# A second stage whose first four weight units take x times the scales of both norms, with the norms' factor behind the bank

## The chip, the core and the metric

One core of a Trainium2 chip runs the whole program in one launch. The metric is the device time of one execution in microseconds (us), the median over several runs. All times in this text are in us unless marked ns. PE is the matmul engine (PEld its weight loads), DVE the vector engine, ACT the scalar engine, POOL GpSimd, SP the queue that loads the weights.

## The reference, cut to what matters

The program is a first block of two layers (feed-forward, mixer, feed-forward) on 256 tokens of width 1024, then a second block. The last operation of the first block is a norm with gain `final_g`; the second block begins with a norm and a modulation, and projects:

```
x = rms_norm(x, final_g)                        # end of the first block
h = _modulate(_rms_norm(x, g_norm_mix), sh1, sc1)
proj = h @ w_in                                 # (256 x 1024) @ (1024 x 3352)
r_q, r_k, r_v, r_g, n_q, n_kc, n_vc, n_ks, n_vs, n_kw, n_vw, n_gate = split(proj)
x = x + ga1 * mix                               # mix: retention and sparse attention of these
```

`_modulate(h, shift, scale)` is `h * (1 + scale) + shift`. Both norms divide each token by a root of its mean square, so for a token t and a channel c, h = x[t, c] * gain[c] * r[t] + shift[c], with one factor r[t] for both norms and one gain for both.

## The kernel before

**Layout and products.** Activations lie with channels on the 128 partitions, in KT = 8 tiles of 128 channels by 256 tokens (columns). Every fp32 product is made of three fp32r matmuls (`product`, lines 283 to 285): hi by hi, hi by lo, lo by hi, where hi is the value rounded to fp32r and lo is the rest. Weights stream in units of 128 x 1024 (512 KB) through a ring of four slots. For each half of a unit (0 and 1: four channel tiles each), ACT rounds it (`Stream.round`, line 175), DVE subtracts (`subtract`, line 182, or POOL from unit 10 of the second stage on, `subtract_beside`, line 235), and PE multiplies. There are two hi and two lo buffers, so that unit u can be rounded only when PE has used the same half of unit u-2 (the semaphore `used`). A unit of the second stage is `chunk` (line 192): 8 channel tiles by 3 matmuls of 256 columns. The first two units are a `pair` (line 258): for each channel tile, three matmuls into each of two banks, as the operand's tiles arrive.

**The end of the last feed-forward.** Its last eight units are products of six hidden tiles (18 matmuls each). Behind unit n, DVE adds the product to x (line 1173), ACT squares the tile of x (`square`, line 487), and PE sums the squares over channels into bank 7, twice, plain and with `final_g` squared (`DoubleNorm.sum`, line 600). The order is written out by hand in `Ffn.tensor`, `scalar` and `vector` (lines 1066 to 1184). `gather` (line 592) is empty for this norm.

**DoubleNorm and the start of the second stage.** PE issues 5 filler matmuls (`keep_warm`, line 385), the last sum, 6 fillers; DVE works out the means (613 to 615), ACT the root (621), DVE the reciprocal (626), and PE spreads the factor over the partitions by 4 matmuls (`spread`, line 633), then 7 fillers. Each filler and each spread appears as two instructions. Then for each channel tile DVE scales (`scale`, 544: x * gain * r into h), ACT rounds (553: h + shift into operand_hi) and DVE subtracts (`split`, 561: operand_lo), in `operands`, a scale ahead of each split. `Second.tensor` runs `pair` on units 0 and 1 (banks 0 and 6), then units 2 to 7 one by one. Their outputs are 128 channels each: compression keys, compression values, selection keys, window keys, four query tiles. ACT evicts each two units with one or two copies (lines 2043, 2044, 1959) and, behind the first two, makes four shifted copies of the compression values (`turned_values`, 1967 and 1968). DVE writes the normed x for the residual (`x2`, line 644), two tiles behind each of units 2 to 5. Behind unit 5 PE rotates the keys (`rotate`, line 1701) and DVE applies the positions (`rope`, 2135 to 2137). Units 8 to 15 are token-wise (activations as the stationary operand); from 16 on, units interleave with attention.

## Time and profile before

| | us |
|---|---|
| three runs | 2800.55, 2800.92, 2805.89 |
| median | 2800.92 |
| profiled execution, own time | 2799.17 |
| its span | 2797.3 |
| PE busy in the span | 2732.1 (98%) |
| end of the last feed-forward to the first product of the second stage | about 1751.4 to 1757.7 |
| mean granted clock of PE | 0.994 |

The profiled execution is 1.87 us over its span, and 1.75 us under the median. A timeline row gives the start from the span's start, the duration, engine, line, operation and tiles, the form and the count, and in brackets how long that engine had been idle and what released it. Rows of one instruction overlap the next where the engine is pipelined: what an instruction occupies is the distance from its start to the next start, and what a follower waits for is its end. PE rows that follow without a wait start 0.12 us apart for 256 columns, while each shows 0.28.

### The profile page before, as it was taken

Reading aid. Unit: us, or ns where it says so; the run is one execution under the profiler, and the core shown is the slowest. Engines: PE = TensorE matmul, PEld = TensorE weight load, DVE = VectorE, ACT = ScalarE, POOL = GpSimd, SP = SyncE. Lnnn points to the kernel's source line nnn. Section 1 sums busy time; section 2 is a strip of 40 time slices with the busy share of each in tenths; the row PEclk is TensorE's granted clock in tenths of the full one; section 3 lists DMA queues with packets and bytes.
Section 4 is the critical chain, followed back from the end, with each engine's and each line's share of the span. In section 5 each row is a group of like instructions: output and inputs, shape, how many; then the busy total and the mean of one; then the engine's idle time right before and its main releaser. Section 6 shows DMA issues by size and latency. Waiting matters only on the chain.

```text
span 2797.3 us, 40204 instructions
## 1 busy us (share of the span) xinstructions
PE 2732.1 (98%) x15618; PEld 2320.2 (83%) x15618; DVE 2067.0 (74%) x3773; ACT 1216.9 (44%) x2228; POOL 522.2 (19%) x449
## 2 busy tenths in 40 slices
PE   7999999999999999999988999999999999999998
PEld 5888878668888878888885999889999888888887
DVE  6989895568989896564766766765896677777776
ACT  5323233453232342222445545565556444444444
POOL 1111114300111101010050000345898000000000
PEclk9999999999999999999999999999999999999999
DMA  7555533223555445354441566424654556655554
GB/s 290 194 186 192 185 136 112 76 103 123 202 182 190 175 154 189 122 191 145 146 148 45 191 216 216 146 84 151 197 152 121 185 190 192 192 193 190 190 190 132
DMA packets 123261, 462.50 MB, mean 165 GB/s; under 512 B 13504, under 2 KB 26688, under 8 KB 109888
## 3 DMA queue, kind: packets, MB, share of 16 engines
q1 hardware_dynamic: 109248, 359.27, 39.5%
q0 software_dynamic: 13824, 100.67, 9.3%
q8 instruction: 124, 2.03, 0.3%
q14 instruction: 65, 0.53, 0.1%
HBM read 452.93 MB, written 6.95 MB: 164 GB/s over the span
## 4 chain that ended last, share of the span: by engine, by line
PE 90%; DVE 7%; issue 1%; ACT 1%; DMA 1%; POOL 1%; POOLq 0%; DVEq 0%; ACTq 0%
PE bank L283 28%; PE bank L284 27%; PE bank L285 27%; PE bank L2469 2%; DVE weight_lo L182 1%; DVE extension_ffn L920 1%; DVE nmax L1397 1%; DMA extension_ffn<-in_w_mods 1%; DVE arena L544 1%; PE bank L940 1%; PE bank L941 1%; PE bank L385 0%; PE bank L508 0%; DVE extension_mixer L1390 0%; POOL weight_lo L235 0%
## 5 line engine op out<-in xcount | busy, mean ns | idle before, releaser
L175 ACT ACTIVATE weight_hi<-weight_ring 128x512 fp32r<-128x512 f32 x1272 | 798.7, 631 | 1188.2 <-PE bank L285 1187.1
L182 DVE TENSOR_TENSOR weight_lo<-weight_ring,weight_hi 128x512 fp32r<-128x512 f32 x1110 | 839.4, 760 | 430.6 <-ACT weight_hi L175 428.9
L283 PE MATMUL bank<-operand_hi,weight_hi 128*128 128x256 f32 (+1 forms) x3168 | 1045.4, 330 | 16.8 <-DVE operand_lo L561 5.6
L284 PE MATMUL bank<-operand_lo,weight_hi 128*128 128x256 f32 (+1 forms) x3168 | 1032.8, 326 | 0.0
L285 PE MATMUL bank<-operand_hi,weight_lo 128*128 128x256 f32 (+1 forms) x3168 | 1032.6, 326 | 0.0
L283 PEld LDWEIGHTS bank<-operand_hi,weight_hi 128*128 128x128 f32 x3168 | 602.2, 190 | 86.1 <-issue 16.1
L284 PEld LDWEIGHTS bank<-operand_lo,weight_hi 128*128 128x128 f32 x3168 | 602.6, 190 | 53.1 <-issue 0.5
L285 PEld LDWEIGHTS bank<-operand_hi,weight_lo 128*128 128x128 f32 x3168 | 602.1, 190 | 50.4
L920 DVE SCALAR_TENSOR_TENSOR extension_ffn<-extension_ffn,silu_c 128x512 f32<-128x512 f32 x532 | 388.4, 779 | 1.7
L235 POOL TENSOR_TENSOR weight_lo<-weight_ring,weight_hi 128x512 fp32r<-128x512 f32 x162 | 211.6, 1315 | 421.1 <-ACT weight_hi L175 418.3
L283 PE MATMUL bank<-hidden_hi_ffn,weight_hi 128*128 128x512 f32 (+1 forms) x704 | 256.6, 364 | 4.0 <-DVE arena L1173 4.0
L285 PE MATMUL bank<-hidden_hi_ffn,weight_lo 128*128 128x512 f32 (+1 forms) x704 | 255.3, 363 | 0.0
L284 PE MATMUL bank<-hidden_lo_ffn,weight_hi 128*128 128x512 f32 (+1 forms) x704 | 255.3, 363 | 0.0
L283 PE MATMUL bank<-weight_hi,act_hi_experts 128*128 128x512 f32 x512 | 214.3, 419 | 0.1
L284 PE MATMUL bank<-weight_lo,act_hi_experts 128*128 128x512 f32 x512 | 200.5, 392 | 0.0
L285 PE MATMUL bank<-weight_hi,act_lo_experts 128*128 128x512 f32 x512 | 200.2, 391 | 0.0
L871 POOL DMA_DIRECT2D extension_ffn<-in_w_mods x88 | 53.6, 612 | 681.3 <-DVE extension_ffn L920 585.2
L887 POOL TENSOR_TENSOR mod_lo_ffn<-extension_ffn,mod_hi_ffn 128x1024 fp32r<-128x1024 f32 (+1 forms) x44 | 98.3, 2233 | 428.0 <-ACT mod_hi_ffn L929 428.0
L283 PEld LDWEIGHTS bank<-hidden_hi_ffn,weight_hi 128*128 128x128 f32 x704 | 132.9, 189 | 28.4 <-DVE arena L1173 6.7
L285 PEld LDWEIGHTS bank<-hidden_hi_ffn,weight_lo 128*128 128x128 f32 x704 | 132.9, 189 | 20.8
L284 PEld LDWEIGHTS bank<-hidden_lo_ffn,weight_hi 128*128 128x128 f32 x704 | 132.9, 189 | 20.6
L283 PEld LDWEIGHTS bank<-weight_hi,act_hi_experts 128*128 128x128 f32 x512 | 95.9, 187 | 37.9 <-DVE act_lo_experts L293 12.3
(280 smaller groups left out, 2543.5 us busy)
## 6 DMA issues: line engine op xcount, KB each, us to landing
weight_ring<-in_ffn SPq DMA_DIRECT2D x272, 512.0 KB, 3.5
weight_ring<-in_experts SPq DMA_DIRECT2D x256, 512.0 KB, 3.5
extension_ffn<-in_w_mods POOLq DMA_DIRECT2D x96, 1024.0 KB, 7.6
weight_ring<-in_w_mix SPq DMA_DIRECT2D x56, 512.0 KB, 3.4
weight_ring<-in_w_second SPq DMA_DIRECT2D x52, 512.0 KB, 3.6
spill<-early_retrieve SPq DMA_DIRECT2D x45, 128.0 KB, 3.9
arena<-spill SPq DMA_DIRECT2D x45, 128.0 KB, 3.5
extension_mixer<-in_rel_bias SPq DMA_DIRECT2D x2, 1536.0 KB, 6.7
```

The source lines that it names most:

```text
L175: nc.scalar.activation(self.hi[:, g % 2, h], self.ring[:, g % NS, h], ACT.Copy).then_inc(self.rounded, 1)
L182: self.nc.vector.tensor_tensor(self.lo[:, g % 2, h], self.ring[:, g % NS, h], self.hi[:, g % 2, h].bitcast(F32), ALU.subtract).then_inc(se ...
L235: self.nc.gpsimd.tensor_tensor(self.lo[:, g % 2, h], self.ring[:, g % NS, h], self.hi[:, g % 2, h].bitcast(F32), ALU.subtract).then_inc(se ...
L283: nc.tensor.matmul(out, a_hi, b_hi, start=start and n == 0, stop=False)
L284: nc.tensor.matmul(out, a_hi, b_lo, start=False, stop=False)
L285: last = nc.tensor.matmul(out, a_lo, b_hi, start=False, stop=stop and n == len(pairs) - 1)
L544: nc.vector.scalar_tensor_tensor(self.h[:, kt, lo:hi], self.x[:, kt, lo:hi], self.gain(kt, g), self.rstd(lo, hi), ALU.mult, ALU.mult).then ...
L871: pool.dma_start(self.w[:, j, u, :, :], src).then_inc(self.loaded[j].sem, 16)
L887: nc.gpsimd.tensor_tensor(self.lo[:, 0:n], self.flat(j), self.hi[:, 0:n].bitcast(F32), ALU.subtract)\
L920: ins = nc.vector.scalar_tensor_tensor(acc, w, scale, acc, ALU.mult, ALU.add)
L940: nc.tensor.matmul(out, pick, self.hi[:, g * 512:(g + 1) * 512], start=(d in (0, self.early) and g == 0), stop=False)
L2469: mm = nc.tensor.matmul(chip.bank[4 + b % 3][:, j * NK:(j + 1) * NK], hots[:, j, 0, :], hots[:, j, 1, :], start=True, stop=True)
```

## The change

Units 0 to 3 of the second stage take `x * gain` (both scales, no factor r and no shift) as their operand. It is made while the last feed-forward runs: ACT rounds each tile behind its square (`round_raw`), DVE subtracts (`split_raw`), into the unused right half of the hidden buffers. Two more columns of the same operand hold the shift, so that each output bank receives x * gain @ w in 256 columns and shift @ w in two more. The sum of the last tile, and the spreading of r, stand inside the pair (`late_pair`, behind channel tiles 2 and 4); all fillers around this norm are gone. Behind each of the four units DVE multiplies the bank by r (`scaled`) and ACT adds the shift's column (`shifted`). Units 4 to 31 still take the full operand, whose scale, round and split are now interleaved by hand with the weights' rounds and subtractions (`late_scalar`, `late_vector`). `turned_values` stands behind the fourth eviction, `x2` behind units 4 and 5. To have room for the two columns, the rows of the 512-wide operand and hidden buffers of the whole first block are 514 long. The diff, without new semaphores and names:

```diff
+def late_pair(units, pe, outs, norm):
+
+    nc = units.nc
+    for kt in range(KT):
+        i = kt // (KT // 2)
+        if kt % (KT // 2) == 0:
+            w = [units.half(pe, 0, j, i) for j in range(2)]
+        pe.wait_ge(norm.raw_in.sem, norm.raw_in.at(kt + 2))
+        b = slice(kt * P - i * HALF, (kt + 1) * P - i * HALF)
+        for j in range(2):
+            last = product(nc, outs[j], [((w[j][0][:, b], w[j][1][:, b]), norm.raw_operand(kt))], start=(kt == 0), stop=(kt == KT - 1))
+            if j == 0 and kt % (KT // 2) == KT // 2 - 1:
+                last.then_inc(units.used, 1)
+        if kt == 2:
+            norm.sums(pe)
+        if kt == 4:
+            norm.spread(pe)
+    last.then_inc(units.used, 2)
+
...
 
 
         sb = lambda name, shape, dt: ctx.enter_context(self.nc.sbuf_tensor(f"{name}_{width}", shape, dt))
-        self.hi, self.lo = sb("operand_hi", [P, KT, width], F32R), sb("operand_lo", [P, KT, width], F32R)
+        pad = 2 if width > S else 0
+        hi, lo = (sb(f"operand_{part}", [P, KT, width + pad], F32R) for part in ("hi", "lo"))
+        self.hi, self.lo, self.raw = hi[:, :, 0:width], lo[:, :, 0:width], (hi[:, :, width - S:], lo[:, :, width - S:])
         self.arena, self.words = sb("arena", [P, words], F32), words
...
+    def round_raw(self, act, kt):
+
+        nc, hi = self.chip.nc, self.raw[0]
+        if kt == 0:
+            nc.scalar.activation(hi[:, :, S:S + 2], self.columns, ACT.Copy).then_inc(self.raw_rounded.sem, 1)
+        nc.scalar.activation(hi[:, kt, 0:S], self.x[:, kt, 0:S], ACT.Copy, scale=self.gain(kt, 0)).then_inc(self.raw_rounded.sem, 1)
+
+    def split_raw(self, dve, kt):
+
+        nc, (hi, lo) = self.chip.nc, self.raw
+        if kt == 0:
+            dve.wait_ge(self.raw_rounded.sem, self.raw_rounded.at(1))
+            nc.vector.tensor_tensor(lo[:, :, S:S + 2], self.columns, hi[:, :, S:S + 2].bitcast(F32), ALU.subtract)\
+                .then_inc(self.raw_in.sem, 1)
+        dve.wait_ge(self.raw_rounded.sem, self.raw_rounded.at(kt + 2))
+        nc.vector.scalar_tensor_tensor(lo[:, kt, 0:S], self.x[:, kt, 0:S], self.gain(kt, 0), hi[:, kt, 0:S].bitcast(F32),
+                                       ALU.mult, ALU.subtract).then_inc(self.raw_in.sem, 1)
+
+    def copy_rstd(self, dve):
+        self.chip.nc.vector.tensor_copy(self.chip.rs[:, :], self.rstd(0, S)).then_inc(self.rs_there.sem, 1)
+        dve.wait_ge(self.rs_there.sem, self.rs_there.at(1))
+
+    def late_scalar(self, act, units, evict):
+
+        units.round(act, 0, 2, [0])
+        self.round_one(act, 0, 0)
+        self.round_one(act, 1, 0)
+        units.round(act, 0, 2, [1])
+        units.round(act, 0, 3, [0])
+        self.round_one(act, 2, 0)
+        evict(0)
+        self.round_one(act, 3, 0)
+        evict(1)
+        self.round_one(act, 4, 0)
+        units.round(act, 0, 3, [1])
+        self.round_one(act, 5, 0)
+        self.round_one(act, 6, 0)
+        units.round(act, 0, 4, [0])
+        self.round_one(act, 7, 0)
+        evict(2)
+        units.round(act, 0, 4, [1])
+        units.round(act, 0, 5, [0])
+        evict(3)
+        units.round(act, 0, 5, [1])
+
+    def late_vector(self, dve, units, evict, middle=None):
+
+        units.subtract(dve, 0, 2, [0])
+        self.scale(dve, 0, 0)
+        self.scale(dve, 1, 0)
+        self.split(dve, 0, 0)
+        self.scale(dve, 2, 0)
+        self.split(dve, 1, 0)
+        units.subtract(dve, 0, 2, [1])
+        units.subtract(dve, 0, 3, [0])
+        self.copy_rstd(dve)
+        evict(0)
+        self.scale(dve, 3, 0)
+        self.split(dve, 2, 0)
+        evict(1)
+        self.scale(dve, 4, 0)
+        self.split(dve, 3, 0)
+        if middle:
+            middle()
+        units.subtract(dve, 0, 3, [1])
+        self.scale(dve, 5, 0)
+        self.split(dve, 4, 0)
+        self.scale(dve, 6, 0)
+        self.split(dve, 5, 0)
+        self.scale(dve, 7, 0)
...
+        self.split(dve, 6, 0)
+        units.subtract(dve, 0, 4, [0])
+        self.split(dve, 7, 0)
+        evict(2)
+        units.subtract(dve, 0, 4, [1])
+        units.subtract(dve, 0, 5, [0])
+        evict(3)
+        units.subtract(dve, 0, 5, [1])
 
...
+            if self.raw:
+                self.round_raw(act, kt)
             return
         if self.after:
             act.wait_ge(self.after.sem, self.after.at(self.first + kt + 1))
         nc.scalar.activation(self.h[:, kt, 0:t], self.x[:, kt, 0:t], ACT.Square).then_inc(self.squared.sem, 1)
+        if self.raw:
...
     def gather(self, dve, kt):
 
         nc, t = self.chip.nc, self.width
+        if self.raw:
+            if kt == 1:
+                self.split_raw(dve, 0)
+            self.split_raw(dve, kt)
         dve.wait_ge(self.squared.sem, self.squared.at(kt + 1))
         if kt > 1:
...
+    def round_one(self, act, kt, g):
+
+        act.wait_ge(self.scaled.sem, self.scaled.at(kt + 1))
+        self.chip.nc.scalar.activation(self.hi[:, kt, 0:S], self.h[:, kt, 0:S], ACT.Identity, bias=self.shift(kt, g))\
+            .then_inc(self.h_ready.sem, 1)
+
...
     def split(self, dve, kt, g):
 
         nc, n = self.chip.nc, len(self.groups)
         lo, hi = self.groups[g]
         dve.wait_ge(self.h_ready.sem, self.h_ready.at(n * kt + g + 1))
-        return nc.vector.scalar_tensor_tensor(self.lo[:, kt, lo:hi], self.h[:, kt, lo:hi], self.shift(kt, g),
+        last = nc.vector.scalar_tensor_tensor(self.lo[:, kt, lo:hi], self.h[:, kt, lo:hi], self.shift(kt, g),
                                               self.hi[:, kt, lo:hi].bitcast(F32), ALU.add, ALU.subtract)
+        if self.raw:
+            last.then_inc(self.split_in.sem, 1)
+        return last
 
...
     def gather(self, dve, kt):
-        pass
+        if kt == 1:
+            self.split_raw(dve, 0)
+        self.split_raw(dve, kt)
...
     def sums(self, pe):
-        self.chip.keep_warm(pe, self.spare, 5)
         self.sum(pe, KT - 1)
 
...
     def spread(self, pe):
         c, nc = self.chip, self.chip.nc
-        c.keep_warm(pe, self.spare, 6)
         pe.wait_ge(self.inverted.sem, self.inverted.at(1))
         for b in (2, 3, 0, 1):
             last = nc.tensor.matmul(c.bank[7][:, b * P:(b + 1) * P], c.rstd4[:, b:b + 1].to_broadcast([P, P]), c.ident[:, :],
                                     start=True, stop=True)
         last.then_inc(self.rstd_there.sem, 1)
-        c.keep_warm(pe, self.spare, 7)
 
...
 def take_for_ffn(chip, ctx, name):
-    part = ([P, max(HIDDEN), T2], F32R)
+    part = ([P, max(HIDDEN), T2 + 2], F32R)
...
+        self.late_scaled = chip.late_scaled.take(4)
+        self.late_tiles, self.late_banks = (N_KC, N_VC, N_KS, N_KW), (0, 6, 1, 2)
...
 
-        norm.sums(pe)
-        norm.spread(pe)
-        units.pair(pe, [bank[0][:, 0:S], bank[6][:, 0:S]], x, norm.split_in)
-        for j in range(2, 8):
+        late_pair(units, pe, [bank[0][:, 0:S + 2], bank[6][:, 0:S + 2]], norm)
+        for j in range(2, 4):
+            units.chunk(pe, 0, j, bank[j - 1][:, 0:S + 2], norm.raw_operand)
+        for j in range(4, 8):
             if j >= 4 and j % 2 == 0:
                 pe.wait_ge(self.evicted.sem, self.evicted.at(j // 2 - 1))
-            units.chunk(pe, 0, j, bank[j // 2 % 2][:, j % 2 * S:(j % 2 + 1) * S], x)
+            units.chunk(pe, 0, j, bank[j // 2 % 2][:, j % 2 * S:(j % 2 + 1) * S], x, ready=norm.split_in if j == 4 else None)
             if j == 5:
...
+        def shifted(n):
+            act.wait_ge(self.late_scaled.sem, self.late_scaled.at(n + 1))
+            out = u[:, self.late_tiles[n], :]
+            last = nc.scalar.activation(out, out, ACT.Identity, bias=chip.late_bias[:, n:n + 1])
+            if n % 2:
+                last.then_inc(self.evicted.sem, 1)
+            if n == 3:
+                turned_values()
+
         self.norm.root(act)
-        self.norm.round(act)
-        for k in range(4):
+        self.norm.late_scalar(act, units, shifted)
+        for k in range(2, 4):
             units.round(act, 0, 2 * k + 2)
             units.round(act, 0, 2 * k + 3, [0])
             act.wait_ge(units.used, units.used_at(2 * k + 1))
-            if k == 0:
-                nc.scalar.activation(u[:, N_KC, :], bank[0][:, 0:S], ACT.Copy)
-                nc.scalar.activation(u[:, N_VC, :], bank[6][:, 0:S], ACT.Copy).then_inc(self.evicted.sem, 1)
-            else:
-                lo = (N_KS, N_Q, N_Q + 2)[k - 1]
-                evict(k, k % 2, u[:, lo:lo + 2, :])
+            lo = (N_Q, N_Q + 2)[k - 2]
+            evict(k, k % 2, u[:, lo:lo + 2, :])
             units.round(act, 0, 2 * k + 3, [1])
-            if k == 0:
-                turned_values()
         for j in range(8, 12):
             units.round(act, 0, j + 2)
...
+        def scaled(n):
+            dve.wait_ge(units.used, units.used_at(n))
+            nc.vector.tensor_copy(chip.late_bias[:, n:n + 1], bank[self.late_banks[n]][:, S:S + 1])
+            nc.vector.tensor_tensor(u[:, self.late_tiles[n], :], bank[self.late_banks[n]][:, 0:S], chip.rs[:, :], ALU.mult)\
+                .then_inc(self.late_scaled.sem, 1)
+
+        norm.split_raw(dve, KT - 1)
         norm.means(dve)
         norm.invert(dve)
-        norm.operands(dve)
-        for j in range(6):
+        norm.late_vector(dve, units, scaled)
+        for j in range(4, 6):
             units.subtract(dve, 0, j + 2)
-            if j < 4:
-                norm.x2(dve, 2 * j)
-                norm.x2(dve, 2 * j + 1)
+            for kt in range(4 * (j - 4), 4 * (j - 3)):
+                norm.x2(dve, kt)
         dve.wait_ge(self.table.sem, self.table.at(16))
         rope(0, 2)
         units.subtract(dve, 0, 8)
...
             ffn.then = DoubleNorm(chip, x, h, ffn.added, 2 * KT, lambda kt: chip.col("final_g", kt, 1))
+            ffn.then.begin_raw([chip.extra[f"hidden_{part}"][:, :, T2 - S:] for part in ("hi", "lo")],
+                               chip.mod2[:, 0:KT].unsqueeze(2).to_broadcast([P, KT, 2]))
         with ExitStack() as second:
```

## Rows read from the trace of the kernel before

**Rows 1.** The page: busy time of the engines; the chain that ended last.

```profile
PE 2732.1 (98%) x15618; PEld 2320.2 (83%) x15618; DVE 2067.0 (74%) x3773; ACT 1216.9 (44%) x2228; POOL 522.2 (19%) x449
...
PE 90%; DVE 7%; issue 1%; ACT 1%; DMA 1%; POOL 1%; POOLq 0%; DVEq 0%; ACTq 0%
```

**Rows 2.** Windows: us, PE, PEld, DVE, ACT, POOL busy (instructions), PEclk, DMA share, GB/s.

```profile
1755.00:1760.00 5.00, 4.84 (x42) 4.66 (x40) 3.82 (x10) 2.40 (x5) 0.00 (x0) 1.00 0.20 71
...
1770.00:1780.00 10.00, 10.00 (x79) 9.46 (x78) 7.50 (x13) 4.84 (x9) 0.00 (x0) 1.00 0.70 224
```

**Rows 3.** Timeline, 1749.9 to 1757.7: start us, us, engine, line, tiles [idle before].

```profile
1749.94 0.42 ACT L487 ACTIVATE arena<-arena 128x256 f32<-128x256 f32 x1 [0.49 <-DVE arena L1173]
...
1750.75 1.29 ACT L175 ACTIVATE weight_hi<-weight_ring 128x512 fp32r<-128x512 f32 x2 [0.40 <-PE bank L285]
...
1751.42 0.69 DVE L182 TENSOR_TENSOR weight_lo<-weight_ring,weight_hi 128x512 fp32r<-128x512 f32 x1 [0.92 <-ACT weight_hi L175]
...
1752.54 0.42 ACT L487 ACTIVATE arena<-arena 128x256 f32<-128x256 f32 x1 [0.49 <-DVE arena L1173]
...
1753.01 0.61 PE L600 MATMUL bank<-one_gain,arena 128*128 128x2 f32 x4
...
1754.35 0.18 DVE L626 RECIPROCAL rstd<-root 128x4 f32<-128x4 f32 x1 [0.27 <-ACT root L621]
...
1754.89 1.06 PE L633 MATMUL bank<-ident,rstd 128*128 128x128 f32 x8
...
1755.99 0.87 DVE L544 SCALAR_TENSOR_TENSOR arena<-arena,gain_both,bank 128x256 f32<-128x256 f32 x2 [1.47 <-PE bank L633]
...
1756.51 0.91 ACT L553 ACTIVATE operand_hi<-arena,mod 128x256 fp32r<-128x256 f32 x2 [2.19 <-DVE arena L544]
...
1757.05 0.48 DVE L561 SCALAR_TENSOR_TENSOR operand_lo<-arena,mod,operand_hi 128x256 fp32r<-128x256 f32 x1 [0.19 <-ACT operand_hi L553]
...
1757.68 0.36 PE L283 MATMUL bank<-operand_hi,weight_hi 128*128 128x256 f32 x1 [0.16 <-DVE operand_lo L561]
```

**Rows 4.** Timeline of PE: end of the pair, end of unit 5.

```profile
1763.60 0.28 PE L284 MATMUL bank<-operand_lo,weight_hi 128*128 128x256 f32 x1
...
1763.72 0.28 PE L285 MATMUL bank<-operand_hi,weight_lo 128*128 128x256 f32 x1
...
1775.24 0.28 PE L285 MATMUL bank<-operand_hi,weight_lo 128*128 128x256 f32 x1
```

**Rows 5.** Timeline of ACT behind the pair.

```profile
1765.79 0.41 ACT L1967 ACTIVATE arena<-arena 64x256 f32<-64x256 f32 x1
...
1767.50 1.67 ACT L175 ACTIVATE weight_hi<-weight_ring 128x512 fp32r<-128x512 f32 x3
```

**Rows 6.** Timeline of DVE, from the pair to the first attention scores.

```profile
1765.74 1.28 DVE L182 TENSOR_TENSOR weight_lo<-weight_ring,weight_hi 128x512 fp32r<-128x512 f32 x2
...
1784.37 0.42 DVE L2135 TENSOR_TENSOR arena<-bank,arena 128x256 f32<-128x256 f32 x1
...
1804.88 0.42 DVE L2189 SCALAR_TENSOR_TENSOR arena<-bank,arena 128x256 f32<-128x256 f32 x1 [4.15 <-PE bank L1770]
```

**Rows 7.** Timeline of POOL, token-wise units of the second stage.

```profile
1791.10 16.95 POOL L235 TENSOR_TENSOR weight_lo<-weight_ring,weight_hi 128x512 fp32r<-128x512 f32 x12 [0.82 <-ACT weight_hi L175]
```

**Rows 8.** Timeline of PE at two long gaps elsewhere in the span.

```profile
592.80 0.47 PE L283 MATMUL bank<-operand_hi,weight_hi 128*128 128x512 f32 x1 [2.02 <-DVE operand_lo L1545]
...
1917.54 0.61 PE L508 MATMUL bank<-ones,arena 128*128 128x2 f32 x4 [2.37 <-DVE arena L495]
```

**Rows 9.** Stages with gaps of PE, columns as in Rows 2 (PEclk: granted clock).

```profile
592.00:595.00 3.00, 2.20 (x10) 1.84 (x11) 3.00 (x6) 3.00 (x7) 0.00 (x0) 1.00 0.03 8
...
1427.00:1434.00 7.00, 4.19 (x31) 3.84 (x32) 7.00 (x5) 2.06 (x5) 5.66 (x3) 1.00 0.28 91
...
1915.00:1923.00 8.00, 5.63 (x35) 5.28 (x34) 4.89 (x13) 2.71 (x7) 0.00 (x0) 0.79 0.70 251
```

**Rows 10.** Line 940, weight loads from windows that begin every 4 bytes: ns min/median/max.

```profile
L940 PEld LDWEIGHTS bank<-mod_hi_ffn,pick_pooling x76: 106/108/108, 83.2 to 1391.5; 128*32 128x32 f32 x76
```

17 lines of the change are left out of this document (14 added, 3 removed).

## The prediction

> **What bounds the kernel now.** I read the page first: PE is busy 98% of the span and holds 90% of the chain that ended last [rows 1]. So only what makes PE wait, or gives it less to do, can move the end. Then the windows around the start of the second stage: PE reads as busy there too, 4.84 of 5.00 us [rows 2], but the timeline shows with what: fillers. So I followed the chain in the timeline. The last weight half that the first product needs ends at 1751.42 + 0.69 = 1752.11. The last square ends at 1752.96, the last sum at 1753.62, the reciprocal at 1754.53, the spread at 1755.95, then a scale, a round and a split, and the first product starts at 1757.68 [rows 3]. Between 1752.1 and 1757.7 PE waits for the norm. The pair ends at 1764.00, unit 5 at 1775.52 [rows 4]; after the start PE never waits until the token-wise units, where POOL's subtractions pace it [rows 7]. DVE then has 4.15 us of idle time before the first attention scores [rows 6], so a DVE that ends its positions a little later holds nobody there. I take the end of unit 5 as the measuring point: behind it the order of work on PE and ACT is as before, everything is released by the engines themselves, and a shift there should reach the end whole.
>
> **Durations.** PE: 0.12 per matmul of 256 columns, 1.44 per half unit, 2.88 per unit; a restart after a wait comes 0.13 behind its releaser and costs 0.08 more in the first matmul [rows 3, 4]. DVE: a 256-column operation with a gain occupies 0.395 and ends after 0.48 [rows 3], a weight subtraction occupies 0.60 and ends after 0.69 [rows 6]. ACT: a 256-column operation with a bias occupies 0.41 and ends after 0.51 [rows 3], a weight round 0.52 and 0.63, each of the four copies of `turned_values` 0.42 [rows 5]. Handing over to ACT or DVE takes 0.04.
>
> **Part 1, raw operands under the feed-forward.** Eight rounds (0.41 each) and eight subtractions (0.395) are added, one pair for each of the last units, plus one small operation each. A unit lasts 2.60 us (1749.94 to 1752.54); in it ACT is idle 0.49 + 0.40 and DVE 0.92 beside other waits [rows 3]. The new round sits between a square and the weight round, 1750.3 to 1750.7, before the weight round's start at 1750.75. Cost nothing while this cover holds; if it didn't, at most 7 x 0.1 us. For the last tile, ACT rounds behind the last square, to 1753.4, and DVE ends its split at 1753.9, before PE comes to that tile at about 1758.9.
>
> **Part 2, the pair starts early.** It now waits only for the weights: 1752.11 + 0.13 = 1752.24, 5.44 earlier than 1757.68. It needs 48 x 0.12 = 5.76 and 0.08, and holds the last sum (0.45) and the spread (0.98, from its 1.06 [rows 3] without the drain). The end of its last product is 1752.24 + 7.27 + 0.16 = 1759.67 against 1764.00: **-4.33**. The spread needs the reciprocal: the sum ends at 1754.9, and the steps to the reciprocal take 0.91 (1753.62 to 1754.53), so 1755.9, while PE reaches the spread at about 1756.4. It does not wait. Fillers (18, 36 instructions) go, but all stood in the same wait, so they give nothing of their own.
>
> **Part 3, 258 columns.** Two more of 256 cost under 1% of 0.12 on 96 matmuls: 0.1 or less (0.03 behind the pair).
>
> **Part 4, the norm's work is now woven into units 2 to 5.** Before, sixteen operand operations of DVE ran under the pair. Now they, the copy of r (0.30 to 0.4, no row; I take the nearest one-source form) and four times a bias copy and a bank multiplication (0.12 + 0.33; the multiplication [rows 6], the small one estimated between 0.08 and 0.16) stand in one queue with the weight subtractions. I wrote both queues out in order from the spread's end, 1757.43:
> - Unit 2: subtracted by 1757.1 and 1760.7, PE needs the halves at 1759.5 and 1761.0: no wait.
> - Unit 3, second half: ahead of it DVE has 9 operand operations (3.56), 2 weight subtractions (1.20), copy and handover (0.44), two multiplications (0.90) and about 0.6 of waits for ACT: to 1764.1. ACT rounds the half only at 1764.31 to 1764.94, for that round stands behind the operand round of tile 4, which stands behind the second shift. DVE ends it at 1765.67, PE goes on at 1765.80, and was ready at 1763.85: **+1.95**.
> - Unit 4, first half: six more operand operations (2.37) stand ahead of its subtraction, which ends at 1768.64; PE at 1768.78, ready at 1767.33: **+1.45**.
> - Unit 4, second half: DVE's last split and third multiplication, ACT's shift, round, DVE's subtraction to 1771.31; PE at 1771.44, ready at 1770.30: **+1.14**.
> - Unit 5, second half: the fourth multiplication ends at 1772.36; ACT shifts (0.41), then does `turned_values` (1.70) before the round, done at 1775.14; subtraction to 1775.87; PE at 1776.00, ready at 1774.40: **+1.60**. Before, these four copies ran behind the pair, where units 2 and 3 were rounded in time.
> - Four restarts add 4 x 0.08 = 0.32.
>
> **Moved steps and queues.** `x2` (8 x 0.395) goes behind units 4 and 5. DVE then is 2.5 us later at the positions than before and PE 2.2, so the 4.15 of idle time shrinks by 0.3. No DMA is added. SP's loads wait for subtractions three units back; units 2 and 3 are subtracted earlier than before, and the unit that is later (5) has three loaded units ahead of it.
>
> **Sum:** -4.33 + 1.95 + 1.45 + 1.14 + 1.60 + 0.32 + 0.03 = **+2.2** at unit 5, and at the end. Against the profiled execution: 2799.17 + 2.2 = 2801.4. The median of the runs stands 1.75 above that execution, so I predict 2800.9 + 2.2 = **2803.1**. The price of a perfect weave bounds it from below: without any wait the sum is -4.3.
>
> **Rivals.** About 0.2%, 5.6 us, is what a measurement of this kernel can tell from no change.
> 1. *The weave costs half as much.* Each wait above is a difference of two chains of ten to fifteen steps on in-order queues; steps of 0.3 instead of 0.4 on DVE, or an ACT that is early where I have it late, halve the 6.1 of waits. For it: PE never lets the subtraction wait more than one round today. Against it: unit 3's and unit 5's waits follow from the written order alone (four copies before a round). -4.3 + 3.2 = -1.1: 2799.8. Chance 0.18.
> 2. *PE's clock falls in the new gaps.* After 2.37 us of idle PE the stretch 1915 to 1923 shows a mean granted clock of 0.79 [rows 8, 9], which is a good 3 us at 1.2 instead of 2.4 GHz. After 2.02 us of idle it stayed at 1.00, and so it did with 4.19 busy of 7 us in several gaps [rows 8, 9]. My gaps are 1.0 to 1.8 of idle after the matmul's own end, four in 11 us, and no filler is left. If it falls once, about 3.4 us (0.21 x 8 x 2) pass at half rate: 1.7 us lost, less what a wait hides. Total +3.9: 2804.8. Chance 0.15. The Trainium skill, "TensorE: Matmul & The Clock Gate", section "What's actually happening", speaks against this change: it says that the throttled state is the default and that only activity releases it. By it the time would be this rival's, 2804.8; the trace agrees so far that the rate fell behind 2.37 us of idle PE and not behind shorter gaps.
> 3. *Slower: the padded rows.* Rows of 514 instead of 512 begin every 8 bytes, in all operands of the first block: 4 feed-forwards of 44 x 24 + 22 x 24 matmuls and 2 mixers of 672, 7,680 in all. If a row that begins off a wider boundary cost PE one more column (0.12 / 256 = 0.47 ns), that is 3.6 us, and with the forecast +5.8: 2806.7, slower. It decides from 0.45 ns per matmul on. Against: weight loads that begin every 4 bytes take 106 to 108 ns whatever their start [rows 10]. No row shows a moving operand so. Chance 0.05.
> 4. *The early start fails,* because a raw tile comes late or the feed-forward is stretched by the added work. For it nothing but the narrow slack of part 1. +3 to +6 more. Chance 0.02.
>
> **Numbers.** Forecast 0.60 with its own range of 2801.3 to 2804.8 (the small operations at both ends, and 0.5 on each side for the waits). Range for 8 in 10: from 2799.0, just below rival 1, to 2806.5, above rival 2 with the long end of my unknowns; a stall-free weave (2796.6) and the padded rows' longer prices lie outside. Faster by over 0.2% would need -5.6, more than the stall-free sum gives: 0.01. Slower by over 0.2%: rivals 3 and 4 and the top of rival 2: 0.07. Within: 0.92.
>
> **What would show it.** The pair's first product 5.4 us earlier relative to the last square, no filler; ACT and DVE busier but PE unchanged before the pair; the sum and spread inside the pair. Waits of PE for DVE's weight subtraction in units 3, 4, 4 and 5, with some 6 us in all, where 1770 to 1780 now reads 10.00 of 10 [rows 2]. Granted clock 1.00 from 1750 to 1780. Matmuls of the first block as long as before. I am wrong in the sum if these waits hold under 4 or over 8 us, in the mechanism if the pair doesn't start before the spread, and in the passing-on if the shift at unit 5 isn't the shift at the end.

## The result and the profile after

The kernel with the change takes **2830.72 us** (median of 4 runs, 2827.80 to 2830.86) against 2801.69 for the kernel before on the same chip: a ratio of 1.0103, 95% interval 1.0091 to 1.0115. The prediction was 2803.1, with 2806.5 as the upper end of its range. It is wrong by 28 us: a change that was called neutral costs 1%.

The page first. The same two lines as [rows 1]:

```profile
PE 2757.7 (97%) x15582; PEld 2318.6 (82%) x15582; DVE 2075.7 (73%) x3791; ACT 1219.5 (43%) x2238; POOL 521.2 (18%) x449
...
PE 90%; DVE 7%; ACT 1%; issue 1%; DMA 1%; POOL 0%; POOLq 0%; DVEq 0%; ACTq 0%
```

PE has 36 instructions fewer (the fillers) and is busy 25.6 us longer (2732.1 before). Outside that, the span holds 71.1 us in which PE is not busy, where before it held 65.2. So most of the loss is not waits: the matmuls themselves take longer. Now the last square of the feed-forward and the second stage, in the timeline of the kernel after (columns as in [rows 3]):

```profile
1780.64 0.36 PE L303 MATMUL bank<-hidden_hi_ffn,weight_hi 128*128 128x258 f32 x1 [0.51 <-DVE weight_lo L182]
...
1780.97 0.42 ACT L603 ACTIVATE arena<-arena 128x256 f32<-128x256 f32 x1 [0.51 <-DVE arena L1303]
...
1782.88 0.50 PE L733 MATMUL bank<-one_gain,arena 128*128 128x2 f32 x4
1784.78 1.05 PE L764 MATMUL bank<-ident,rstd 128*128 128x128 f32 x8
...
1793.91 0.39 PE L303 MATMUL bank<-hidden_hi_ffn,weight_hi 128*128 128x258 f32 x1 [1.57 <-DVE weight_lo L182]
1796.92 0.35 PE L303 MATMUL bank<-operand_hi,weight_hi 128*128 128x256 f32 x1 [1.30 <-issue]
1799.46 0.39 PE L303 MATMUL bank<-operand_hi,weight_hi 128*128 128x256 f32 x1 [0.87 <-DVE weight_lo L182]
1803.97 0.39 PE L303 MATMUL bank<-operand_hi,weight_hi 128*128 128x256 f32 x1 [1.38 <-DVE weight_lo L182]
...
1805.71 0.60 ACT L2091 ACTIVATE arena<-bank 128x512 f32<-128x512 f32 x1 [0.96 <-PE bank L305]
```

Three things are to be seen. The last square starts at 1780.97, where before it was 1752.54 [rows 3]: **28.4 us are lost before the second stage begins**, in a part of the program that the change seemed to touch only by the length of some rows. From that square to ACT's eviction of unit 5 it takes 24.74; before, 1775.56 - 1752.54 = 23.02, the eviction from this row of the kernel before:

```profile
1775.56 0.60 ACT L1959 ACTIVATE arena<-bank 128x512 f32<-128x512 f32 x1 [0.75 <-PE bank L285]
```

So the rebuilt second stage costs 1.72 up to that point; the forecast was 2.2. And its four waits stand where they were forecast. The windows of PE there, columns as in [rows 2]:

```profile
1780.00:1790.00 10.00, 9.49 (x80) 9.43 (x80) 7.04 (x17) 4.46 (x10) 0.00 (x0) 1.00 0.36 108
1790.00:1800.00 10.00, 6.26 (x48) 5.67 (x47) 8.19 (x23) 5.83 (x12) 0.00 (x0) 1.00 0.32 105
1800.00:1806.00 6.00, 4.62 (x36) 4.17 (x35) 3.18 (x9) 4.54 (x10) 0.00 (x0) 1.00 0.40 131
```

From 1790 to 1800 PE is busy 6.26 of 10 us, where the kernel before was busy 10.00 of 10 in 1770 to 1780 [rows 2]. The granted clock stays at 1.00 in every window.

Where the 28.4 us are is seen in the groups of PE's products, shape by shape. Behind the bar stand the busy time in us and the mean of one in ns. The kernel before:

```profile
L283 PE MATMUL bank<-operand_hi,weight_hi 128*128 128x512 f32 x1280 | 501.2, 392 | 5.9 <-DVE operand_lo L711 2.7 <-DVE operand_lo L1545 2.0 <-DVE operand_lo L561 1.0
L285 PE MATMUL bank<-operand_hi,weight_lo 128*128 128x512 f32 x1280 | 498.9, 390 | 0.0
L284 PE MATMUL bank<-operand_lo,weight_hi 128*128 128x512 f32 x1280 | 498.8, 390 | 0.0
L285 PE MATMUL bank<-hidden_hi_ffn,weight_lo 128*128 128x512 f32 x528 | 205.5, 389 | 0.0
L284 PE MATMUL bank<-hidden_lo_ffn,weight_hi 128*128 128x512 f32 x528 | 205.5, 389 | 0.0
```

The same groups of the kernel after. The last one has 256 columns, and took 283 before too:

```profile
L303 PE MATMUL bank<-operand_hi,weight_hi 128*128 128x512 f32 x1280 | 508.2, 397 | 7.3 <-DVE operand_lo L841 2.7 <-DVE operand_lo L689 2.5 <-DVE operand_lo L1675 2.0
L305 PE MATMUL bank<-operand_hi,weight_lo 128*128 128x512 f32 x1280 | 506.5, 396 | 0.0
L304 PE MATMUL bank<-operand_lo,weight_hi 128*128 128x512 f32 x1280 | 505.9, 395 | 0.0
L305 PE MATMUL bank<-hidden_hi_ffn,weight_lo 128*128 128x512 f32 x528 | 208.9, 396 | 0.0
L304 PE MATMUL bank<-hidden_lo_ffn,weight_hi 128*128 128x512 f32 x528 | 208.7, 395 | 0.0
...
L305 PE MATMUL bank<-operand_hi,weight_lo 128*128 128x256 f32 x1856 | 525.0, 283 | 0.0
```

Every 512-wide product of the first block is 5 to 7 ns longer. A stretch of 70 us in which PE never waits says it without the overlap of neighbours (windows 445 to 515, before, then after; the first number in brackets is PE's matmuls):

```profile
445.00:515.00 70.00, 70.00 (x310) 57.98 (x309) 31.98 (x26) 22.28 (x39) 50.52 (x35) 1.00 0.31 98
```

```profile
445.00:515.00 70.00, 70.00 (x303) 56.77 (x303) 31.06 (x27) 23.64 (x41) 44.14 (x31) 1.00 0.30 98
```

70 us by 310 are 225.8 ns, by 303 231.0. From here on I give the mean distance from one matmul's start to the next. It is worked out from the start times in the traces, over all matmuls of weight products that follow each other without a wait; no view prints it. In the first block, 512 columns: 226.9 before, 232.2 after. There are (1,280 + 528) x 3 = 5,424 of them: 5,424 x 5.3 = 28.7 us. That is the loss.

### The profile page after: what moved, and what is told of

It reads as the page before. It is cut to its first block, busy times and chain, and to the rows that moved or that the text cites. A ratio compares the mean times of both kernels' runs of the same rounds, so it can differ in the third digit from the quotient of the medians.

```text
span 2828.8 us, 40162 instructions
## 1 busy us (share of the span) xinstructions
PE 2757.7 (97%) x15582; PEld 2318.6 (82%) x15582; DVE 2075.7 (73%) x3791; ACT 1219.5 (43%) x2238; POOL 521.2 (18%) x449
## 4 chain that ended last, share of the span: by engine, by line
PE 90%; DVE 7%; ACT 1%; issue 1%; DMA 1%; POOL 0%; POOLq 0%; DVEq 0%; ACTq 0%
PE bank L303 28%; PE bank L305 27%; PE bank L304 27%; PE bank L2610 2%; DVE weight_lo L182 2%; DVE extension_ffn L1050 1%; DVE arena L666 1%; DVE nmax L1527 1%; DMA extension_ffn<-in_w_mods 1%; PE bank L1071 1%; PE bank L1070 1%; PE bank L630 1%; ACT weight_hi L175 0%; DVE operand_lo L689 0%; PE bank L1498 0%
## 5 line engine op out<-in xcount | busy, mean ns | idle before, releaser
L303 PEld LDWEIGHTS bank<-operand_hi,weight_hi 128*128 128x128 f32 x3136 | 595.5, 190 | 96.9 <-issue 18.5
L303 PE MATMUL bank<-hidden_hi_ffn,weight_hi 128*128 128x512 f32 (+2 forms) x736 | 267.9, 364 | 5.3 <-DVE arena L1303 3.2
L305 PE MATMUL bank<-hidden_hi_ffn,weight_lo 128*128 128x512 f32 (+2 forms) x736 | 267.9, 364 | 0.0
L304 PE MATMUL bank<-hidden_lo_ffn,weight_hi 128*128 128x512 f32 (+2 forms) x736 | 267.4, 363 | 0.0
L303 PEld LDWEIGHTS bank<-hidden_hi_ffn,weight_hi 128*128 128x128 f32 x736 | 138.7, 189 | 32.8 <-DVE arena L1303 5.9
L304 PEld LDWEIGHTS bank<-hidden_lo_ffn,weight_hi 128*128 128x128 f32 x736 | 138.8, 189 | 23.8
L305 PEld LDWEIGHTS bank<-hidden_hi_ffn,weight_lo 128*128 128x128 f32 x736 | 138.7, 188 | 22.4
```

The source lines that it names most:

```text
L303: nc.tensor.matmul(out, a_hi, b_hi, start=start and n == 0, stop=False)
L304: nc.tensor.matmul(out, a_hi, b_lo, start=False, stop=False)
L305: last = nc.tensor.matmul(out, a_lo, b_hi, start=False, stop=stop and n == len(pairs) - 1)
```

## The experiments

Times are medians; a ratio is against the kernel before in the same group of runs, with its 95% interval.

### First group: what is it in the first block?

**Rows alone.** The kernel before with only the longer rows (operand and hidden buffers):

```diff
-        self.hi, self.lo = sb("operand_hi", [P, KT, width], F32R), sb("operand_lo", [P, KT, width], F32R)
+        pad = 2 if width > S else 0
+        hi, lo = (sb(f"operand_{part}", [P, KT, width + pad], F32R) for part in ("hi", "lo"))
+        self.hi, self.lo = hi[:, :, 0:width], lo[:, :, 0:width]
...
-    part = ([P, max(HIDDEN), T2], F32R)
+    part = ([P, max(HIDDEN), T2 + 2], F32R)
```

> The kernel before, with only the rows of the 512-wide operand and hidden buffers made 514 long. Theory R (row length): the 28 us lost before the second stage come from the longer rows, because the 512-wide matmuls of the first block then start 232 ns apart instead of 227: about 2829 us, ratio 1.010. Theory B (bases): the two new small buffers (1056 bytes) moved the base address of every buffer behind them, and that is what the matmuls feel: then this kernel is at 1.000. Theory W (the new work itself, at the end of the feed-forward and in the second stage): 1.000 too.

Measured: 2828.3, ratio 1.0096 [1.0079, 1.0113]; 232.2 ns. The rows alone make the loss.

**Bases alone.** The change also takes 1,056 bytes ahead of all these buffers, and ahead of the weights' buffers too:

```diff
+        self.rs, self.late_bias = sb("rs", [P, S]), sb("late_bias", [P, 4])
```

> The kernel before, with only the two new small buffers (256 and 4 columns) allocated and never used, which moves every later buffer by 1056 bytes. Theory R: 1.000, and 512-wide matmuls 227 ns apart. Theory B: 1.010, 232 ns apart. Theory W: 1.000.

Measured: 2800.88, ratio 1.0002 [0.9992, 1.0011]; 226.9 ns. It is not that all bases moved together.

**Rows of 528 words** in the changed kernel, so that each row begins at a multiple of 64 bytes from the first:

```diff
-        pad = 2 if width > S else 0
+        pad = 16 if width > S else 0
...
-    part = ([P, max(HIDDEN), T2 + 2], F32R)
+    part = ([P, max(HIDDEN), T2 + 16], F32R)
...
-            ffn.then.begin_raw([chip.extra[f"hidden_{part}"][:, :, T2 - S:] for part in ("hi", "lo")],
+            ffn.then.begin_raw([chip.extra[f"hidden_{part}"][:, :, T2 - S:T2 + 2] for part in ("hi", "lo")],
```

> The changed kernel with rows of 528 instead of 514, so that each row begins at a multiple of 64 bytes from the buffer's base. Theory R in the form that rows must begin on a boundary: 1.001, the 28 us come back and what is left is the change's own part, +1.7 to +3 us. Theory R in the form that any row other than 512 is slow: 1.010. Theory B: 1.010, as the bases are those of the changed kernel. Theory W: 1.010.

Measured: 2828.42, ratio 1.0098 [1.0081, 1.0115]; 231.8 ns. Rows that begin every 64 bytes are hardly cheaper than rows that begin every 8 (232.2).

**The change without the rows.** All rows 512 long but the hidden buffers of the last feed-forward, whose products are 256 wide:

```diff
-        pad = 2 if width > S else 0
+        pad = 0
...
-def take_for_ffn(chip, ctx, name):
-    part = ([P, max(HIDDEN), T2 + 2], F32R)
+def take_for_ffn(chip, ctx, name, pad=0):
+    part = ([P, max(HIDDEN), T2 + pad], F32R)
...
+                    take_for_ffn(chip, sublayer, f"ffn{l}1", 2 * l)
```

> The changed kernel with rows of 512 everywhere but in the hidden buffers of the last feed-forward, which alone hold the raw operand; the matmuls there are 256 wide. Theory R in both forms: 1.001, that is +1.7 to +3 us over before, the change's own part. Theory B: 1.010. Theory W: 1.010.

Measured: 2803.13, ratio 1.0009 [1.0000, 1.0019]: +2.4 us. The timeline and PE's waits from 1750 to 1830:

```profile
1754.22 0.42 ACT L603 ACTIVATE arena<-arena 128x256 f32<-128x256 f32 x1 [0.63 <-DVE arena L1303]
...
1778.97 0.60 ACT L2091 ACTIVATE arena<-bank 128x512 f32<-128x512 f32 x1 [0.95 <-PE bank L305]
```

```profile
PE bank L303 <- DVE weight_lo L182: 4.5, 4, 1.6
PE bank L303 <- POOL weight_lo L235: 1.9, 3, 0.7
PE bank L303 <- issue: 1.3, 1, 1.3
```

24.75 from the last square to the eviction, +1.73 against before: as in the changed kernel. (The last square itself lies between 1752.5 and 1754.6 in the profiled executions of kernels whose first block is that of before; so one execution can't show 1 us in the whole, and I compare distances.) What remains of the change without its rows is +2.4 where +2.2 was forecast.

### Second group: why do longer rows cost?

In the kernel before, the sizes of the buffers put the weights and every row of operand and hidden tiles at the same place of a 256-byte grid. This, and every distance below, is worked out from the sizes; no profile shows an address. Longer rows undo that in several ways at once: rows against the weights, lo rows against hi rows, each row against the next. These kernels undo them one by one; all are the kernel before, otherwise unchanged. The letters A to C now stand for three new theories, which the first expectation states: A, rows against the weights; B, hi against lo rows, or tile against tile; C, the length of a row.

```diff
gap_weights
+        if width > S:
+            sb("gap", [P, 16], F32)
         self.hi, self.lo = sb("operand_hi", [P, KT, width], F32R), sb("operand_lo", [P, KT, width], F32R)
gap_hi_lo
         self.hi = sb("operand_hi", [P, KT, width], F32R)
+        if width > S:
+            sb("gap", [P, 16], F32)
         self.lo = sb("operand_lo", [P, KT, width], F32R)
...
-hidden_hi=part, hidden_lo=part
+hidden_hi=part, gap=([P, 16], F32), hidden_lo=part
operand_514: the operand's part of rows_only
hidden_576
-    part = ([P, max(HIDDEN), T2], F32R)
+    part = ([P, max(HIDDEN), T2 + 64], F32R)
```

> The kernel before with 64 unused bytes between the weight buffers and the operand buffers; all rows stay 512 words. In the kernel before, the rows of weights, operand and hidden buffers all begin at the same place of a 256-byte (even 2048-byte) grid; here all moving rows begin 64 bytes beside the weights' place. Theory A (PE pays where moving rows and stationary weights don't begin at the same place of that grid): 512-wide matmuls go from 226.7 to about 232 ns start to start, 2801 + 28 = 2829. Theory B (what costs is that hi and lo rows of one tile differ in their place, or that rows of successive tiles do): 2801. Theory C (what costs is the length of the row, whatever the place): 2801.

> The kernel before with 64 unused bytes between operand_hi and operand_lo and 64 between hidden_hi and hidden_lo; rows of 512 words. The hi row of the operand begins at the weights' place, its lo row 64 bytes beside it. Theory A (place against the weights): of three matmuls of an operand product one has its rows beside the weights' place, of a hidden product all three (hidden_hi is moved by 64, hidden_lo by 128 bytes): 1,280 x 5.1 ns + 1,584 x 5.1 ns = 14.6 us, 2815. Theory B (hi against lo, which follow each other in a product): all 5,424 pay, 2829. Theory C (the length of the row alone): 2801.

> Rows of 514 words in the operand buffers alone, 512 in the hidden ones. Any theory in which the operand's 3,840 512-wide matmuls pay 5.1 ns each: + 19.6 us, 2820, with the hidden ones at 226.7 ns under theory C and the theory of hi against lo (hidden_hi and hidden_lo stand at the same place of the grid here), but at 232 under theory A, since the hidden buffers begin 128 bytes beside the weights' place: 2829.

> Rows of 576 words (2304 bytes, nine times 256) in the hidden buffers alone, 512 in the operand. Theory of the place on a 256-byte grid, A or B: every row still begins at the same place of it, so nothing is paid: 2801. Theory C (any length other than 512 words): 1,584 x 5.1 ns = 8.1 us, 2809.

| kernel | beside the weights' place: operand hi, lo; hidden hi, lo (bytes) | us | ratio |
|---|---|---|---|
| gap_weights | 64, 64; 64, 64 | 2809.71 | 1.0035 [1.0023, 1.0047] |
| gap_hi_lo | 0, 64; 64, 128 | 2826.58 | 1.0094 [1.0077, 1.0111] |
| operand_514 | 0 and 64, and 8 more per tile; 128, 128 | 2827.77 | 1.0096 [1.0080, 1.0113] |
| hidden_576 | 0, 0; 0, 0 | 2800.68 | 1.0005 [0.9995, 1.0015] |

The hidden tiles' groups in the kernel with rows of 576, then in the one with operand rows of 514:

```profile
L284 PE MATMUL bank<-hidden_lo_ffn,weight_hi 128*128 128x512 f32 x528 | 205.5, 389 | 0.0
L285 PE MATMUL bank<-hidden_hi_ffn,weight_lo 128*128 128x512 f32 x528 | 205.5, 389 | 0.0
```

```profile
L285 PE MATMUL bank<-hidden_hi_ffn,weight_lo 128*128 128x512 f32 x528 | 208.4, 395 | 0.0
L284 PE MATMUL bank<-hidden_lo_ffn,weight_hi 128*128 128x512 f32 x528 | 208.3, 395 | 0.0
```

The first says that the length of a row is nothing in itself: 576 words cost 0 where 514 cost 5 ns. **Theory C falls.** The second says that rows of exactly 512 words pay in full (232.4 ns) when they lie 128 bytes beside the weights' place. So it is the place, and theory A's sign is right. Its price is not one number: with everything 64 bytes beside, 512 columns take 229.3, half of what A said, and the total is 2809.7 instead of 2829. With hi and lo at different places too (gap_hi_lo) they take 232.0, though two thirds of the operand's matmuls lie at the weights' place; B expected that, A 2815. Those two thirds are the sharpest evidence: the hi rows have not moved against the weights, and yet their groups take 396 and 395 where the kernel before took 392 and 390:

```profile
L283 PE MATMUL bank<-operand_hi,weight_hi 128*128 128x512 f32 x1280 | 507.0, 396 | 7.3 <-DVE operand_lo L714 2.7 <-DVE operand_lo L564 2.5 <-DVE operand_lo L1548 2.0
L285 PE MATMUL bank<-operand_hi,weight_lo 128*128 128x512 f32 x1280 | 505.1, 395 | 0.0
```

So neither theory alone gives both kernels: the place against the weights counts, and so does the place against the rows of the neighbouring matmuls.

gap_weights held something nobody had expected. Its groups of 256 columns, against 283 and 534.1 us before:

```profile
L285 PE MATMUL bank<-operand_hi,weight_lo 128*128 128x256 f32 x1888 | 531.7, 282 | 0.0
L284 PE MATMUL bank<-operand_lo,weight_hi 128*128 128x256 f32 x1888 | 531.7, 282 | 0.0
```

A small step in a mean over the whole program; but the gap exists in the first block alone, and in the last feed-forward the distance from start to start fell from 119.9 to **117.3** ns. The same 64 bytes that make a 512-wide matmul slower make a 256-wide one quicker.

### Third group: is it the distance, and does it pay to use it? And is the weave's cost the written order?

Three of these are the kernel before. all_by_64 puts 64 bytes ahead of the weights too. second_apart puts them ahead of the second stage's operand alone; x lies in both stages' arenas, so the first block's arena is moved as well, and a gap of 192 bytes brings the hidden buffers back to the weights' place. both_apart adds the last feed-forward, by taking its tiles from column 16 of their rows on:

```diff
all_by_64
+        ctx.enter_context(nc.sbuf_tensor("gap", [P, 16], F32))
         self.ring = ctx.enter_context(nc.sbuf_tensor("weight_ring", [P, NS, UNIT], F32))
second_apart
+        if width == S:
+            sb("gap", [P, 16], F32)
         self.hi, self.lo = sb("operand_hi", [P, KT, width], F32R), sb("operand_lo", [P, KT, width], F32R)
+        if width > S:
+            sb("gap", [P, 16], F32)
         self.arena, self.words = sb("arena", [P, words], F32), words
...
-A_FFN, hidden_hi=part
+A_FFN, gap=([P, 48], F32), hidden_hi=part
...
-"experts", act_hi
+"experts", gap=([P, 48], F32), act_hi
both_apart, beside that
+                    if last:
+                        chip.hi, chip.lo = chip.hi[:, :, 16:16 + S], chip.lo[:, :, 16:16 + S]
+                        for part in ("hidden_hi", "hidden_lo"):
+                            chip.extra[part] = chip.extra[part][:, :, 16:16 + S]
```

> The kernel before with 64 unused bytes ahead of the weight ring, so that weights, operand and hidden buffers all begin 64 bytes further on, and still at the same place of the 256-byte grid against each other. If it is the place of the moving rows against the weights that made gap_weights slower in 512-wide matmuls (229.3 ns) and quicker in 256-wide ones (117.3 against 119.9), both are as before here: 226.7 and 119.9, 2800. If it is the place of the moving rows in the memory itself, this kernel shows 229.3 and 117.3, about 2810.

> The kernel before with the operand buffers of the second stage alone 64 bytes beside the weights' place (gap_weights showed 117.3 instead of 119.9 ns for 256-wide matmuls there where the buffers were apart, and 229.3 instead of 226.9 for 512-wide ones); first block as before. If the place against the weights sets the time of every matmul: some 4,100 matmuls of 256 columns take 2.5 ns less, some 380 of 512 take 2.4 more, -10.3 + 0.9: 2791. If the second stage is paced by its chains (attention, sorting) rather than by PE, less comes through: 2795 to 2800. If the gain of the 256-wide matmuls in gap_weights belongs to the last feed-forward alone: 2801.

> As second_apart, and the last feed-forward (256-wide) reads and writes its operand and hidden tiles from column 16 of their rows on, 64 bytes beside the weights' place. Some 1,770 more matmuls of 256 columns take 2.5 ns less: another -4.4: 2787 where the whole gain comes through.

Measured: all_by_64 2800.29, ratio 0.9998 [0.9988, 1.0008], with 227.0 and 119.9 ns. So at 64 bytes it is the place against the weights, not the place in the memory. second_apart: 2797.09, ratio 0.9984 [0.9974, 0.9993]; the second stage's 256-wide matmuls 117.9 instead of 119.8. -3.4 us came of the -9.4 that the expectation adds up to. The gain per matmul was 1.9 instead of 2.5, 7.6 us over some 4,000 of them; what took the other 4 us is not shown. In its profiled execution, whose 2800.40 is the longest of its ten, part of the gain went to PE's clock, in this stretch (the kernel before, then this one):

```profile
1920.00:1960.00 40.00, 39.68 (x319) 39.27 (x320) 24.06 (x128) 22.28 (x45) 26.25 (x21) 0.96 0.47 155
```

```profile
1920.00:1960.00 40.00, 38.92 (x302) 38.54 (x303) 22.77 (x114) 20.70 (x42) 23.25 (x19) 0.91 0.44 146
```

0.05 of 40 us is 2.0. This comes with the execution and not with the edit, as far as single executions tell: the stretch 520 to 560, which the edit doesn't touch, also shows 0.91 here and 0.96 before, and both_apart below, with the same edit in the second stage, has 1.00 in 1920 to 1960 and 0.97 in 1860 to 1920. From the last square to the end both_apart's profiled execution is 6.9 shorter than the kernel before's, this one's 2.9.

both_apart: 2793.75, ratio 0.9974 [0.9964, 0.9984]; the last feed-forward at 118.0, another -3.3 (expected -4.4). Size off, direction right.

The weave is on top of the change without rows (pad_last):

```diff
     def late_scalar(self, act, units, evict):
...
         self.round_one(act, 1, 0)
+        self.round_one(act, 2, 0)
         units.round(act, 0, 2, [1])
         units.round(act, 0, 3, [0])
-        self.round_one(act, 2, 0)
+        units.round(act, 0, 3, [1])
         evict(0)
         self.round_one(act, 3, 0)
         evict(1)
         self.round_one(act, 4, 0)
-        units.round(act, 0, 3, [1])
+        units.round(act, 0, 4, [0])
         self.round_one(act, 5, 0)
+        units.round(act, 0, 4, [1])
         self.round_one(act, 6, 0)
-        units.round(act, 0, 4, [0])
         self.round_one(act, 7, 0)
-        evict(2)
-        units.round(act, 0, 4, [1])
         units.round(act, 0, 5, [0])
-        evict(3)
         units.round(act, 0, 5, [1])
+        evict(2)
+        evict(3)
...
-            if n == 3:
-                turned_values()
...
             units.round(act, 0, 2 * k + 3, [1])
+            if k == 2:
+                turned_values()
```

`late_vector` (DVE) follows the same order.

> The change, with rows of 512 words everywhere but in the last feed-forward's hidden buffers (as pad_last), and with the norm's work woven in otherwise: unit 3's second half is rounded and subtracted right behind its first, unit 4's halves ahead of operand tiles 6 and 7, the last two bank multiplications and shifts and turned_values behind unit 5's rounds. If the waits of unit 3 to 5 come from the written order (my steps in the prediction), most of the 5.7 us of waits go: unit 5 ends some 3.5 us earlier than in pad_last, 2799.5, 1.3 below the kernel before. If the queues' total work between the pair and unit 5 is what holds PE, the waits only move: 2802 to 2803.

Measured: 2799.67, ratio 0.9997 [0.9988, 1.0006]. PE's waits from 1745 to 1830:

```profile
PE bank L303 <- POOL weight_lo L235: 2.0, 3, 0.7
PE bank L303 <- DVE weight_lo L182: 1.8, 4, 0.7
PE bank L303 <- issue: 0.5, 1, 0.5
```

5.8 us for DVE and "issue" (DVE's operand tiles) are now 2.3, and from the last square to the eviction of unit 5 it takes 21.44 (1753.70 to 1775.14), 3.3 less than in pad_last. The work is the same and only its order differs, so most of these waits followed from the written order; 2.3 are left.

### Fourth group: one step of the forecast, other distances, and both findings in one

turned_later is pad_last with turned_values alone moved (the last lines of the diff above).

> pad_last (the change with rows of 512 words in the first block) with turned_values alone moved, from behind the fourth shift to behind unit 7's second round. The prediction's step for unit 5's second half (+1.60 for four copies ahead of its round): that wait of PE falls from 1.38 to nothing or 0.1, unit 5 ends 1.5 earlier, 2801.5 against pad_last's 2803.1. If DVE's fourth bank multiplication or the two shifts hold the round as well, the wait only shrinks, and the gain is under 0.8.

Measured: 2800.80, ratio 1.0003 [0.9994, 1.0012]; pad_last, in another group of runs, had 1.0009, so the medians are some 2 us apart, which their intervals cannot tell from nothing. The trace is sharper. Its waits and the eviction of unit 5:

```profile
PE bank L303 <- DVE weight_lo L182: 3.1, 3, 1.6
...
PE bank L303 <- issue: 1.3, 1, 1.3
```

```profile
1776.47 0.60 ACT L2091 ACTIVATE arena<-bank 128x512 f32<-128x512 f32 x1 [0.75 <-PE bank L305]
```

One wait fewer and 1.4 less in all. From the last square (1753.37) it is 23.10 to the eviction, 1.65 less than in pad_last: the step that the prediction priced at 1.60, taken by itself.

Two more distances, in second_apart's diff with 32 and 48 words in the gaps, and the others filled up to 64 words:

> As second_apart, with the second stage's operands 128 bytes beside the weights' place instead of 64. If any place but the weights' own is as good: 117.9 ns for 256-wide matmuls. If it is the amount that matters (operand_514's hidden tiles, 128 bytes beside, took 118.7 in 256-wide and 232.4 in 512-wide ones against 117.3 and 229.3 at 64 bytes): 118.5 to 119.

> As second_apart, with 192 bytes. If the grid is 256 bytes and only the distance counts, 192 is 64 on the other side: 117.9. If the direction counts, anything from 117 to 120.

| second stage's operand beside the weights' place | ns per 256-wide matmul, 1790 to 2300 | us | ratio |
|---|---|---|---|
| 0 bytes (before) | 119.8 | 2800.55 | |
| 64 | 117.9 | 2797.09 (other group) | 0.9984 [0.9974, 0.9993] |
| 128 | 119.7 | 2802.55 | 1.0005 [0.9995, 1.0015] |
| 192 | 115.1 | 2791.67 | 0.9964 [0.9953, 0.9974] |

128 bytes give nothing, and 192 more than 64. The direction counts; that only the distance does is refuted. It is not the arena (the activations' buffer) either, which moved along with the operands in the kernels of the second group: second_by_192 moves the first block's arena by 192 bytes, and its 512-wide products stay at 227.0.

> weave and both_apart in one kernel: the change with its norm work woven in anew, rows of 512 words but in the last feed-forward's hidden buffers (576), and the 256-wide products' operands 64 bytes beside the weights' place. The two gains are in different terms (waits at units 3 to 5; time per 256-wide matmul) and add up if nothing else becomes the bound: -0.8 and -6.8 against before, 2793.0. If the second stage's chains take back what PE gains, 2795 to 2797.

Measured: 2791.9, ratio 0.9968 [0.9957, 0.9980]. The gains add, as far as an interval of 3 us to either side tells: 8.7 below the kernel before, where 7.6 was expected.

### Last group: the best placement, without and with the change

Both as before with 48 words (192 bytes) in place of 16, in the last feed-forward and the second stage; weave_by_192 has hidden rows of 576 words in the last feed-forward, so that the raw operand lies 192 bytes beside as well.

> The kernel before with the operands of the last feed-forward (from column 48 of their rows on) and of the second stage 192 bytes beside the weights' place; none of the change. second_by_192 gave 2791.7 (115.1 ns for 256-wide matmuls in 1790 to 2300). If the last feed-forward's 1,770 matmuls gain as much, 119.9 to 115.1: another -8.5, 2783. If it gains as in both_apart (-3.3): 2788.

> As both_by_192, with the change in its rewoven form. If the change's own worth (weave: -0.8 against before) is the same with quicker matmuls: 0.8 under both_by_192, 2782. If the norm's work on DVE and ACT, which is no quicker, now holds PE longer between the pair and unit 5, up to 1.5 over it: 2784.

Measured: both_by_192 2782.07, ratio 0.9930 [0.9916, 0.9944]; weave_by_192 **2781.34**, ratio 0.9939 [0.9925, 0.9952], against 2799.8. PE's line of the page in these two:

```profile
PE 2715.1 (98%) x15618; PEld 2301.4 (83%) x15618; DVE 2069.3 (74%) x3773; ACT 1216.5 (44%) x2228; POOL 520.8 (19%) x449
```

```profile
PE 2709.5 (98%) x15582; PEld 2295.2 (83%) x15582; DVE 2073.7 (75%) x3791; ACT 1217.9 (44%) x2238; POOL 521.3 (19%) x449
```

PE is busy 17.0 and 22.6 us less than before [rows 1] for the same products (the second has no fillers and two columns more in four units). The placement is worth 18 us by the medians. Both kernels beat the kernel before and the changed one.

For both_by_192 the 2783 came true, but not for its reason. It rested on 115.1 ns in the last feed-forward, and the trace shows 118.0 there, as at 64 bytes. That is worth 3.3 us: the last square starts at 1749.29, before at 1752.54. From there to the end the profiled execution is 10.7 shorter, 14.0 in all. The median shows 17.7 (the profiled execution is the longest of the five); what makes up the 3.7 between them is not shown.

The change on top of the placement is worth 0.7 by the medians, which these intervals cannot tell from nothing, and that is not the change alone: in weave_by_192 the last feed-forward takes 114.7 ns, and its last square starts at 1744.82.

## Why the prediction was wrong, point by point

**The step that failed.** It is the sum of the change part by part, which has no term for the rows at all, and the claim in its list of signs that matmuls of the first block stay as long as before. The rows stood only in rival 3, at one column, 0.47 ns, "3.6 us", chance 0.05. It looked at the right rows. Its mechanism, a row that begins off a wider boundary, is not what the runs show: all_by_64 moves every row off its 256-byte boundary together with the weights and costs nothing, while operand_514's hidden rows, of exactly 512 words but 128 bytes beside the weights' place, pay in full. What counts is where rows begin against the weights and against each other. The price was 5.3 ns on the 5,424 matmuls of 512 columns and nothing (119.1 against 119.9, a small gain) on those of 256: 28.7 us. Two mistakes made the 0.05. The evidence against it [rows 10] is of weight loads that begin at various places; it shows nothing of a moving row, and the prediction says so in its next sentence and still leans on it. And the price of "one column" was no bound: for a cost that no row shows, the only rows were means of the existing placement, so its upper end was open and should have been taken far higher, multiplied by 7,680. A term with that multiplier and no row needs a wide range more than it needs a good guess.

**What held, at its size.** The pair starts 0.33 ahead of the last square (1780.64 against 1780.97) where the kernel before started 5.14 behind it: 5.47 earlier, forecast 5.44. Sum and spread stand in the pair and hold nobody. The four waits, each as the start of PE's first matmul behind it against 0.12 after the start of the last one ahead of it (1792.07, 1795.34, 1798.31 and 1802.31 in the timeline): 1.72, 1.46, 1.03 and 1.54, forecast 1.95, 1.45, 1.14 and 1.60. In all 5.75 for 6.14, and with it +1.72 at unit 5 for +2.2. pad_last, the change without its rows, has +2.4 at the end. Its interval reaches from 0 to 5 us, so it is the distances in the traces, not this median, that bear the sum out.

**The rivals.** Rival 1 (waits half as large) is refuted by these waits in this order; the reordered weave shows that another order has them, at 2.3. Rival 2 (the clock) did not happen: 1.00 in every window from 1776 to 1806, with four gaps of 0.87 to 1.57 of idle PE. The rule cited from the Trainium skill ("TensorE: Matmul & The Clock Gate", "What's actually happening") did not come to bear on gaps of this size; the prediction had read it too widely when it let it speak for any gap. Rival 4 did not happen: part 1's added work stood in the idle time it was given, and PE's sums behind the last units stand 2.6 us apart in both kernels.

## What to carry to other kernels

A change of a buffer's size or row length can be a change of every instruction that reads the rows behind it: count those instructions first, and give a term without a row a range that is as wide as its multiplier deserves. Where matmuls fill PE, look at where the moving rows begin against the stationary ones, and try places, before any weaving: here that was worth 18 us, the whole weave 3. And copies that nobody waits for go behind the rounds that PE waits for.
